# Experts' down product with the tokens stationary, a transposed router and a paired rotary key, in a two-block transformer kernel

## What is computed

```
# rotary key of the first attention: per head, rows 0..63 from a product, rows 64..95 the shared rotary key
# router
logits = x @ w_router + b                     # 512 x 8
top-2 of 8 experts, softmax over the two
# experts, each on the tokens routed to it (at most 160 slots here, a fallback handles more)
y_e = (silu(x_e @ w_gate[e]) * (x_e @ w_up[e])) @ w_down[e]     # 1024 -> 1408 -> 1024
x = x + sum over the two chosen experts of weight * y_e
```

## Time and profile before

| | us |
|---|---|
| median of 3 runs | 2865.38 (2862.03 to 2868.08) |
| the profiled execution, its own time | 2867.97 |
| its span in the profile | 2866.2 |
| PE busy | 2761.9 |
| mean granted PE clock | 0.985 of full |

### The profile page before, as it was taken

How to read it: one execution, slowest core, us unless ns; L and a number is a source line. 1 busy time by engine, 2 the same in 40 slices (tenths; PEclk the granted TensorE clock), 3 DMA queues, 4 the chain that set the end, 5 groups by cost and what they waited for, 6 DMA issues and landing times.

```text
span 2866.2 us, 37966 instructions
## 1 busy us (share of the span) xinstructions
PE 2761.9 (96%) x14493; PEld 2302.5 (80%) x14493; DVE 1041.9 (36%) x2085; ACT 709.1 (25%) x1768; POOL 1523.5 (53%) x1650
## 2 busy tenths in 40 slices
PE   7999999999999899999999989699999998999999
PEld 3537878888878799999999977578888786788887
DVE  1156633213256310000000235637357237465372
ACT  2247741001110111111111133432112225421120
POOL 2230047767777341414270344368879663588785
PEclk9999999999999899999999999899999999999999
DMA  6821023333342279999999920342332222433331
GB/s 185 187 84 31 1 60 103 95 90 99 121 140 76 73 218 269 271 262 254 253 270 257 272 74 20 108 134 86 107 96 91 87 59 95 117 94 96 103 95 46
DMA packets 526579, 371.09 MB, mean 129 GB/s; under 512 B 15918, under 2 KB 476535, under 8 KB 525754
## 3 DMA queue, kind: packets, MB, share of 16 engines
q1 hardware_dynamic: 507568, 321.58, 39.3%
q0 software_dynamic: 12240, 33.00, 3.8%
q10 hardware_dynamic: 6586, 14.03, 2.0%
HBM read 335.55 MB, written 32.41 MB: 128 GB/s over the span
## 4 chain that ended last, share of the span: by engine, by line
PE 90%; DVE 3%; issue 2%; ACT 2%; DMA 1%; POOL 0%; ACTq 0%; another core or an unknown queue 0%; DVEq 0%; SPq 0%; POOLq 0%
PE bank L600 18%; PE bank L602 18%; PE bank L601 18%; PE bank L760 14%; PE bank L1209 7%; PE bank L876 2%; PE bank L854 2%; PE bank L772 1%; PE bank L864 1%; PE bank L824 1%; PE bank L838 1%; DMA ring<-in_moe_w_up 1%; ACT x_hi L1616 1%; DVE x L2583 1%; DVE x_lo L2446 1%
## 5 line engine op out<-in xcount | busy, mean ns | idle before, releaser
L2065 POOL TENSOR_TENSOR unit_parts<-ring,unit_parts 128x512 fp32r<-128x512 f32 x580 | 806.8, 1391 | 48.4
L2063 POOL TENSOR_SCALAR unit_parts<-ring 128x512 fp32r<-128x512 f32 x580 | 425.6, 734 | 508.8 <-PE bank L602 330.9
L600 PE MATMUL bank<-x_hi,unit_parts 128*128 128x512 f32 x1408 | 554.8, 394 | 19.3 <-DVE x L2583 10.3
L602 PE MATMUL bank<-x_hi,unit_parts 128*128 128x512 f32 x1408 | 550.0, 391 | 0.0
L601 PE MATMUL bank<-x_lo,unit_parts 128*128 128x512 f32 x1408 | 549.7, 390 | 0.0
L760 PE MATMUL bank<-arena,ring 128*128 128x160 f32 x2816 | 388.5, 301 | 5.6 <-ACT arena L1804 3.7
L760 PEld LDWEIGHTS bank<-arena,ring 128*128 128x128 f32 x2816 | 386.0, 191 | 6.3 <-ACT arena L1804 3.9
L600 PEld LDWEIGHTS bank<-x_hi,unit_parts 128*128 128x128 f32 x1408 | 265.5, 189 | 77.4 <-DVE x L2583 11.5
L600 PE MATMUL bank<-unit_parts,hid_parts 128*128 128x512 f32 x784 | 308.1, 393 | 3.2 <-DVE hid_parts L2605 2.6
L602 PEld LDWEIGHTS bank<-x_hi,unit_parts 128*128 128x128 f32 x1408 | 265.3, 188 | 55.7
L601 PEld LDWEIGHTS bank<-x_lo,unit_parts 128*128 128x128 f32 x1408 | 265.4, 188 | 55.2 <-issue 1.0
(11 more groups left out here) (363 smaller groups left out, 3294.9 us busy)
## 6 DMA issues: line engine op xcount, KB each, us to landing
ring<-in_moe_w_gate SPq DMA_DIRECT2D x88, 512.0 KB, 5.5
ring<-in_moe_w_up SPq DMA_DIRECT2D x88, 512.0 KB, 7.0
ring<-in_moe_w_down SPq DMA_DIRECT2D x64, 704.0 KB, 4.8
ring<-in_w_up SPq DMA_DIRECT2D x88, 512.0 KB, 5.3
ring<-in_w_down SPq DMA_DIRECT2D x16, 1024.0 KB, 5.1
ring<-in_od_w_in SPq DMA_DIRECT2D x24, 512.0 KB, 4.5
ring<-in_ffn_w_gate SPq DMA_DIRECT2D x22, 512.0 KB, 4.0
ring<-in_ffn_w_up SPq DMA_DIRECT2D x22, 512.0 KB, 5.3
```

The source lines that it names most:

```text
L600: pe.matmul(ps, a[0], b[0], start=start, stop=False)
L602: return pe.matmul(ps, a[1], b[0], start=False, stop=stop)
L2063: pool.tensor_scalar(hi, raw, 1.0, 1.0, ALU.mult, ALU.mult).then_inc(S("units_rounded"), 1)
L2065: pool.tensor_tensor(lo, raw, hi.bitcast(F32), ALU.subtract).then_inc(S("units_split"), 1)
```

## The change

1. Down product: the tokens become the stationary side. The first 128 slots (`main_rows`) are computed in three fp32r parts against rows of `w_down`, 512 columns each, two banks of features. The other 32 slots (`tail_rows`) stay plain float32: four matmuls of 32 stationary columns, each on another 256 features, which write PSUM rows 0, 32, 64 and 96 onward. The result is token-major: `yT`, its copies and `turn_y` are gone.
2. The split that this needs: ACT rounds each of 11 rows-of-weights (128x1024) into `down_hi`, which has 3 buffers, and each tile of `hidE`; DVE subtracts, the rest of the weights lying in place in the ring slot. A slot is so held until the main product has used it. Down weights are now loaded as 6 chunks of two whole rows.
3. `tail_rows` runs three rows ahead of `main_rows`; the next expert's gather stands between the first three tails and the rest.
4. `store_y` replaces the copies of `turn_y`: 1 + 2 ACT copies and 4 + 2 stores per expert. In the last expert the tail rows lie in four 32-row groups, and `scatter_last` uses 64 rows of them per half.
5. Router: 8 float32 matmuls with 32 stationary columns in four column groups (two rounds) give transposed logits; ACT copies them; four matmuls with a selection matrix `pick` sum and turn them. `places` becomes one matmul of 32 columns, one of 32 on running sums that DVE makes (four small operations), and one of 8. DVE's top-two operations are no longer linked one by one.
6. Rotary key: the copy of `krT` becomes a 128-row, 64-column matmul into PSUM rows 64 to 127; `krT` is cleared by POOL at the start.
7. DVE adds the other experts' rows (`add_results`) during the last expert's up product, no longer after it.

```
             w = chunk((0, KD, 8, A["moe_w_router"][0]), (8 * KD, KD, 8, A["moe_w_router"][0]))
             ps = claim(("logitsT",))
             for k in range(KD):
                 q = 32 * (k % 4)
                 ins = pe.matmul(ps[q:q + 32, :], w[:, k * 8:k * 8 + 32], xnT[:, k, :], start=k < 4, stop=k >= 4)
...
-                    fill(pe.matmul(ps[64:96, :], c("ident")[64:96, 64:96], krT[64:96, :], start=True, stop=True), key)
+                    fill(pe.matmul(ps[64:P, :], c("ident")[:, 64:P], krT[:, :], start=True, stop=True), key)
...
+            def down(e, between):
+                main = [claim(("y", e, n)) for n in range(2)]
+                tail = claim(("y", e, 2))
...
+                def tail_rows(k):
...
+                    for q in range(4):
+                        ins = pe.matmul(tail[32 * q:32 * q + 32, 0:256], hidE[:, k, P:CAP],
+                                        ring[:, at + 256 * q:at + 256 * q + 256], start=k == 0, stop=k == KE - 1)
...
+                def main_rows(k):
+                    n = KE * e + k
+                    pe.wait_ge(S("hidE_split"), n + 1)
+                    pe.wait_ge(S("down_split"), n + 1)
...
+                    for m in range(2):
+                        cols = slice(m * 512, (m + 1) * 512)
+                        pe.matmul(main[m][:, :], h_hi, w_hi[:, cols], start=k == 0, stop=False)
+                        pe.matmul(main[m][:, :], h_hi, w_lo[:, cols], start=False, stop=False)
+                        ins = pe.matmul(main[m][:, :], h_lo, w_hi[:, cols], start=False, stop=k == KE - 1)
...
+                for k in range(TAILS_AHEAD):
+                    tail_rows(k)
+                if between:
+                    between()
+                for k in range(KE):
+                    if k + TAILS_AHEAD < KE:
+                        tail_rows(k + TAILS_AHEAD)
+                    main_rows(k)
...
+            def round_down(e, k):                                   # ACT
+                n = KE * e + k
+                act.wait_ge(*arrived)
+                if n >= DOWN_HI:
+                    act.wait_ge(*down_rows[n - DOWN_HI][3])
+                act.activation(down_hi[:, n % DOWN_HI, :], raw, ACT.Copy).then_inc(S("down_rounded"), 1)
...
+            def split_down(e, k):                                   # DVE
+                dve.wait_ge(S("down_rounded"), n + 1)
...
+                dve.tensor_tensor(lo, raw, down_hi[:, n % DOWN_HI, :].bitcast(F32), ALU.subtract)\
+                   .then_inc(S("down_split"), 1)
```

More of the change, by code:

```diff
@@ L1152, in scatter_last @@
                         ps = claim(key)
[L1153 to L1167, removed]
-                    for q in range(4):
-                        ins = pe.transpose(ps[0:w, q * P:(q + 1) * P], yT[:, 4 * half + q, b * P:b * P + w],
-                                           c("ident"))
-                    fill(ins, ("yb", e, half, b))
+                        at = slice(t * P, (t + 1) * P)
@@ L1198, in _ @@
                 wait_drained(pe, ("xg", e, 2 * PER_BANK))
[L1199 to L1204, removed]
[L1205 to L1217 removed]
+                up_pairs(f"moe{e}", KE, A["moe_w_gate"][0, e], A["moe_w_up"][0, e], xg, CAP)
+                down(e, (lambda e=e: gather(e + 1)) if e + 1 < NE else None)
                 if e in (2, 4):
@@ L1760, in silu_pairs @@
                     drain(act.activation(buf[:, n % 2, :], ps[:, 0:width], ACT.Silu), key)
-                    if j == at and between:
-                        between()
+                    if between:
+                        between(j)
             for half in range(2):
@@ L1796, in _ @@
             norm_stage("od_ffn")
+            ps = wait_filled(act, ("logitsT",))
+            drain(act.activation(logitsT, ps[:, :], ACT.Copy), ("logitsT",))
             act.wait_ge(S("top2_ready"), 1)
@@ L1829, in turn_y @@
                     return
                 if e:
[L1831 to L1840 removed]
+                    act.wait_ge(S("rows_out"), 96 * e)
@@ new lines, in store_y @@
+                drain(act.activation(rows_out[:, 1, 0:256], tail[:, 0:256], ACT.Copy), ("y", e, 2))
+                wait_drained(act, ("y", e, 2))
+                for q in range(4):
+                    act.dma_start(results_dram[at + P:at + CAP, 256 * q:256 * q + 256],
+                                  rows_out[32 * q:32 * q + 32, 1, 0:256]).then_inc(S("rows_out"), 16)
+                for n in range(2):
+                    key, cols = ("y", e, n), slice(n * 512, (n + 1) * 512)
+                    ps = wait_filled(act, key)
+                    drain(act.activation(rows_out[:, 0, cols], ps[:, :], ACT.Copy), key)
+                    wait_drained(act, key)
+                    act.dma_start(results_dram[at:at + P, cols], rows_out[:, 0, cols]).then_inc(S("rows_out"), 16)
@@ L1886, in _ @@
                 elif e == S5_ROUNDS:
-                    for b, w in ((0, P), (1, TAIL)):
+                    for b in range(2):
                         ps = wait_filled(act, ("oh", b))
-                        if b:
-                            act.wait_ge(S("tails_clear"), 3)
-                        drain(act.activation(slotT[0:w, b, :], ps[0:w, :], ACT.Copy), ("oh", b))
-            turn_y(NE - 1, 1)
+                        drain(act.activation(slotT[:, b, :], ps[:, :], ACT.Copy), ("oh", b))
             n_tokens = act.value_load(most_i[0:1, 0:1], min_val=0, max_val=T)
```

279 lines of the change are left out of this document (177 added, 102 removed).

## The result

| | before | after |
|---|---|---|
| median | 2865.03 us (4 runs, 2862.03 to 2868.08) | 2822.34 us (4 runs, 2819.29 to 2823.76) |
| ratio | | 0.985 (0.9832 to 0.9867) |
| span of the profiled execution | 2866.2 | 2820.5 |
| PE busy | 2761.9 | 2725.0 |

The medians differ by 42.7 us where 37.2 were forecast. The two numbers are near each other partly by luck. The experts with their end gave 10 to 12 us less than forecast (some 6 us by the traces and 3.7 us in a run of that part alone, where 26.5 - 7.5 - 2.9 = 16.1 stood), and 15.5 to 16.5 us came from a place in the second block that the prediction never looked at.

What follows compares the result with a forecast made beforehand. PE, busy 2761.9 of 2866.2 us, was taken as the bound. From 2867.97, 26.5 - 7.5 - 2.9 + 14.1 + 7 = 37.2 us less gave 2830.8, and 2828 for the median; forecast 2815 to 2842 (0.62), range 2804 to 2862.

Steps and rivals of the forecast that it cites:

- Tails: Down product's narrow float32 matmuls: four column groups together, 0.43 us per row of weights, 11 x 0.43 = 4.7 us per expert.
- the first three rivals: Tail column groups one after another (2946 us, chance 0.07), two at a time (2866, 0.05), or not wholly together (2846, 0.13).
- Changes of shape: Down product, between tail and full-width matmuls: 0.12 us in, 0.20 out; nine pairs, 2.9 us per expert.
- The fifth rival: Changes of shape in the down product cost nothing, as weight loads get ahead: 2805 us, chance 0.07.
- Main part: Down product's 66 fp32r matmuls of 512 columns per expert, 0.2256 us each: 14.9 us.
- The splits: ACT rounding and DVE subtracting down weights: 7.5 us lost, 4 beside busy POOL, 0.5 and 2 in last expert, 1 elsewhere.
- DVE's multiplies of the next up product come after its splits.: Down product's splits: the step on what is queued behind them on DVE; no cost charged for it.
- Loads: Expert weights stay 16.5 MB, the rate rises by 4%, SP waits for PE: nothing charged.
- End of the experts: Last down product to scatter: 0.9 us of waits for 1.16, scatter 3.2 longer; 2.9 us lost.
- Router: Logits to first gather: 11.4 us in place of 25.5, 14.1 us gained.
- Rotary key: Both matmuls of a head run together, 0.97 of 3.86 us less per head: 7 us gained, bounds 0 and 7.8.
- signs of being wrong: Tails above 0.8 us a row; PE waiting on `down_split` in most experts or for `ring`; low clock beyond the first expert.

Runs made afterwards that it cites:

- run 4: Changed kernel with a row's four tail matmuls in the same 32 columns: 1.0244 of before; with only one of the four: 0.9844.
- run 3: Changed kernel with tails two rows of weights at a time behind the first three: 0.9801 of the kernel before.
- run 2: Changed kernel with `add_skip` moved ahead of the splits, into the fourth and sixth expert's up product: 0.9816 of the kernel before.
- only_router: Kernel before with the router's part of the change alone: 0.9944 of the kernel before, -16.0 us.
- skip_early: Changed kernel with `add_skip` behind the third pair of the fourth and sixth expert's up product: 0.9816 of the kernel before.
- no_return: Changed kernel without POOL's eight indirect loads of the other experts' rows (DVE adds zeros): 0.9828 of the kernel before.
- before_slot_zero: Kernel before with the ring's next slot after the experts set to 0, as the change leaves it: 0.9958 of the kernel before.
- tails_by_two: Changed kernel with tails two rows of weights at a time, 5 changes of shape in and out per expert, not 9: 0.9801 of the kernel before.
- only_rotary: Kernel before with the rotary key's part of the change alone: 0.9978 of the kernel before, -6.3 us.
- one_group_four: Changed kernel with all four tail matmuls of a row of weights in the same 32 columns: 1.0244 of the kernel before, 2935.4 us.
- combo: Changed kernel with `add_skip` early, tails two rows at a time, and POOL's indirect loads spread over the last up product: 0.9777 of before, 2799.9 us.

## Why the prediction was right, and where it was not

- **Tails: right.** 0.43 us a row with four column groups together; run 4 shows it, and the first three rivals fall with their 113, 38 and 18 us.
- **Changes of shape: right.** 0.12 in and 0.20 out forecast, 0.14 and 0.20 measured, and run 3 shows that they belong to the change and not to the row. The rule of the Trainium skill ("TensorEngine Tiling (Array Packing)", Key Properties: a change of mode drains the engine) agrees with the 0.14; by two equal drains the way out would cost as much, and it costs 0.20. In the scatter, with row groups of 64 and 512 columns, both ways cost 0.2. The fifth rival (nothing) falls.
- **Main part: a little undersized.** I took 0.2256 us from 266 records in 60 us. The chain shows 0.23 to 0.24 a matmul (a row of weights takes 2.16 - 0.57 = 1.59 with its first matmul at 0.43). 66 times the difference is 0.4 us an expert, and the gather takes 1.63 in place of 1.48. Together the sum of an expert is 22.9, not 22.5, and 22.4 us are gained over eight where 26.5 were forecast. Why the same form takes 2.5% longer here than in the dense stage of the earlier trace rows stays open.
- **The splits: the term was wrong.** I charged 7.5 us for waits on splits. PE waited 0.5 us for one, once: the first split of the last expert, the one part of the 7.5 that came as forecast. Two rows misled me. The slow subtraction of L3053 beside a busy POOL did not come: L2933's median is 1225 ns, also in the sixth expert, where POOL works for 59 of 73 us. Its longest of 88, 2009 ns, stands beside POOL's splitting for the next stage, as forecast, but holds PE for no more than 0.2 us. And the last three rows, which I called covered by nothing to spare, were covered.
- **What stood in its place is the step that failed**: "DVE's multiplies of the next up product come after its splits." I asked what of the up product was queued behind the splits, and left out `add_skip`, which stands there too, with POOL and then PE waiting for it: 9.5 us at one place (run 2: 9.7). The prediction names what is queued behind the rounding on ACT and who waits for that; on DVE it stops at the multiplies.
- **Loads: wrong at one place.** "Nothing is charged" held for seven experts. In the last one the ring already waited 1.9 us, with the indirect loads on top of the weights; it waits 4.1 now, with the up product at 54.0 us in place of 50.3: 3.7 us. The row was there to be read: PE's busy time of 518 in 520 us leaves just these 1.9 us out.
- **End of the experts: right.** 2.8 us lost where 2.9 were forecast: 0.83 and 10.62 us against 0.9 and 10.7.
- **Router: right, undersized.** 9.5 us against 11.4 forecast; alone it gives 16.0 where 14.1 stood. DVE came from the logits to `routed` in 2.2 us and not 3.4, and the four small matmuls took 1.04 us and not 1.6.
- **Rotary key: right.** 0.96 a head, seven times; 6.3 us alone. DVE stayed in time.
- **The slot number: not seen**, 15.5 us. The diff changes the number of chunks, and slots are handed out in turn for the whole kernel, so every later chunk moves to another slot. Whoever changes how many items go through a ring must look at each later place that treats slots by their number.

The errors cancel: 22.4 + 16.0 + 6.7 + 15.5 - 9.5 - 3.7 - 0.5 - 2.8 = 44.1, where 26.5 + 14.1 + 7 - 7.5 - 2.9 = 37.2 stood. Not in this sum are 0.7 us lost in turning the last expert's slots, and two small waits of PE in the kernel before that are gone: 0.5 us ahead of the last down product and 0.8 behind the scatter. Without the slot's accident the time would have been 2822.3 + 15.5 = 2838, near the upper edge of my 2815 to 2842; that it came within 6 us of my 2828 is luck.

Of the signs named in advance, those on the tails, on L1215 to L1217, on the matmul behind a tail, on the down phase (22.9 us without the gather) and on the heads came. The router's did not (9.5 us, not 11 to 12), nor did the wait of the sixth expert for L2933. Of the signs of being wrong, two came at single places: PE waited for `ring` in the last expert, and the granted clock fell below full behind that wait (0.93 from 1561 to 1585 us) and behind the one for `add_skip`.

## What to carry to other kernels

When an engine gets a new block of work, list everything that stands behind that block in its program, also small operations for a later stage, and follow who waits for each; their place is free to choose and cost 9.5 us here. When a change alters how many items pass through a ring or a set of banks handed out in turn, everything behind it shifts: run the change with the old number too, or its accident is taken for its merit. Narrow matmuls beside full-width ones cost per change of shape, not per matmul, so collect them as far as the ring allows.

## What the runs showed that I had not expected

Three further column groups of PE, each with other moving data, cost 0.02 us beside one of 0.55.

Stretches whose code is unchanged differ between profiled executions by up to 4.4 us where the granted clock differs. From 205 to 260 us (windows, as in the earlier trace rows; the clock is the third number from the end) the kernel before and `only_router`, with the same code there:

```profile
205.00:260.00 55.00, 50.87 (x292) 37.40 (x291) 34.79 (x150) 36.03 (x115) 3.27 (x3) 0.94 0.08 20
```
```profile
205.00:260.00 55.00, 51.03 (x252) 35.66 (x250) 31.11 (x132) 32.61 (x103) 3.27 (x3) 0.84 0.07 20
```

Paired with the kernel before, `only_router` is 1.2 us behind at the start of this stretch and 5.6 at its end, and still 5.6 when its router begins. The 2.6 us of the rotary's gain that were gone again by the router in the trace of after may be of this kind, and so may be what is left between the slot's 15.5 us and the 12 and 15 measured. A part worth under 5 us can't be read from one pair of traces placed side by side; its own place can.

Open: ACT idles 3.4 us ahead of the last copies of the first gather, with no releaser but an unknown one, in the executions of the kernel before, `skip_early`, `no_return` and four others (3.3 to 4.3 us), and for 1.9 us in `before_slot_zero` and `tails_by_two`; it does not in those of after, `only_router`, `only_rotary`, `one_group_four` and `combo`. It comes with either router, so it is no part of what the change gives or takes as far as these traces show. What it is was not tried.
